# A hybrid backbone step on one core: the residual stored without its affine, modulation rows formed earlier, the last tile by halves

## The reference, cut to what matters

```python
x   = layer_norm(x, ln_in_g, ln_in_b)                       # input norm, with its affine
mod = silu(cond) @ w_mod + b_mod                            # six rows of 1024 per condition
shift1, scale1, gate1, shift2, scale2, gate2 = mod
u   = x * (1 + scale1) + shift1
x   = LN1(alpha * x + gate1 * TokenMix(u))                  # mLSTM + Fourier + pooling, merged, one output product
u2  = x * (1 + scale2) + shift2
x   = LN2(alpha * x + gate2 * HierMoE(u2))                  # top-1 group, top-2 of its 4 experts
```

## Time and profile before

| | us |
|---|---|
| median of 3 runs (1083.56, 1078.26, 1077.09) | 1078.26 |
| the profiled execution | 1081.63 |
| span of its trace | 1079.1 |
| PE busy (share of the span) | 998.3 (93%) |
| DVE busy | 664.8 (62%) |
| ACT busy | 445.4 (41%) |
| POOL busy | 172.2 (16%) |

### The profile page before, as it was taken

One profiled execution on the slowest core, in us unless ns is written; L12 is line 12 of the kernel. 1 busy time (PEld: TensorE's weight loads), 2 busy tenths in 40 slices (PEclk: granted clock), 3 DMA queues, 4 the chain that ended last, 5 costly groups with the idle time before them and its releaser, 6 DMA issues.

```text
span 1079.1 us, 13664 instructions
## 1 busy us (share of the span) xinstructions
PE 998.3 (93%) x4723; PEld 781.9 (72%) x4723; DVE 664.8 (62%) x943; ACT 445.4 (41%) x626; POOL 172.2 (16%) x210
## 2 busy tenths in 40 slices
PE   6997999999999999897989998699999999999883
PEld 2687998667777777764657776588888888888741
DVE  5569473024444547346486657786799955799628
ACT  1542221132443424301023013475688853778523
POOL 2133710111000001100212430311120101020030
PEclk6798998999999999998999998999999999999987
DMA  9856162241203102723354124695999988699572
GB/s 333 315 197 247 67 218 87 88 137 20 79 2 117 44 35 98 262 61 109 116 192 158 55 91 165 223 395 189 383 399 399 399 319 292 220 400 397 213 266 117
DMA packets 84967, 213.21 MB, mean 198 GB/s; under 512 B 7040, under 2 KB 7318, under 8 KB 84928
## 3 DMA queue, kind: packets, MB, share of 16 engines
q1 hardware_dynamic: 66000, 149.45, 37.8%
q0 software_dynamic: 14640, 48.51, 13.1%
q10 hardware_dynamic: 4288, 14.72, 3.6%
HBM read 189.54 MB, written 23.11 MB: 197 GB/s over the span
## 4 chain that ended last, share of the span: by engine, by line
PE 79%; DVE 9%; DMA 6%; ACT 3%; issue 2%; SPq 1%; ACTq 0%; POOL 0%; DVEq 0%
PE ps L1972 28%; PE ps L1734 22%; PE ps L1595 6%; PE ps L1720 5%; DMA ring<-in_w_in 2%; PE ps L1849 2%; PE ps L1966 1%; PE ps L1788 1%; DMA ring<-in_w_mod 1%; PE ps L1950 1%; PE ps L1601 1%; DVE w_lo L1169 1%; PE ps L1705 1%; ACT w_hi L848 1%; PE ps L1634 1%
## 5 line engine op out<-in xcount | busy, mean ns | idle before, releaser
L1734 PE MATMUL ps<-w_hi,uT_hi 128*128 128x512 f32 x320 | 132.9, 415 | 4.6 <-ACT R_x L913 2.5
L1734 PE MATMUL ps<-w_lo,uT_hi 128*128 128x512 f32 x320 | 126.7, 396 | 0.0
L1169 DVE TENSOR_TENSOR w_lo<-ring,w_hi 128x1024 fp32r<-128x1024 f32 x52 | 62.9, 1249 | 37.6 <-ACT w_hi L848 35.6
L1734 PEld LDWEIGHTS ps<-w_hi,uT_hi 128*128 128x128 f32 x320 | 60.9, 190 | 22.2 <-issue 5.4
L1408 DVE TENSOR_TENSOR wa_lo<-ring,wa_hi 128x1024 fp32r<-128x1024 f32 x64 | 74.1, 1218 | 0.5
L1734 PEld LDWEIGHTS ps<-w_lo,uT_hi 128*128 128x128 f32 x320 | 60.6, 190 | 13.5
L1972 PE MATMUL ps<-wa_hi,xgT_hi 128*128 128x512 f32 x152 | 62.8, 413 | 6.5 <-DVE xgT_lo L1505 6.5
L848 ACT CAST w_hi<-ring 128x1024 fp32r<-128x1024 f32 x52 | 53.0, 1059 | 34.0 <-PE ps L1734 23.4
L913 ACT ACTIVATE R_x<-ps 128x512 f32<-128x512 f32 x30 | 17.9, 596 | 116.0 <-PE ps L1734 115.9
L1734 PE MATMUL ps<-w_hi,uT_lo_a 128*128 128x512 f32 x160 | 64.1, 400 | 0.0
L1734 PE MATMUL ps<-w_hi,uT_lo_b 128*128 128x512 f32 x160 | 62.4, 390 | 0.0
(11 more groups left out here) (413 smaller groups left out, 2259.9 us busy)
## 6 DMA issues: line engine op xcount, KB each, us to landing
ring<-in_w_up SPq DMA_DIRECT2D x64, 512.0 KB, 9.5
ring<-in_w_in SPq DMA_DIRECT2D x11, 2048.0 KB, 10.1
R_d<-in_w_up SPq DMA_DIRECT2D x32, 512.0 KB, 10.9
R_p<-in_w_down SPq DMA_DIRECT2D x32, 512.0 KB, 9.7
R_h<-in_w_down SPq DMA_DIRECT2D x32, 512.0 KB, 10.3
y_slots<-R_m ACTq DMA_DIRECT2D x19, 512.0 KB, 6.2
ring<-in_w_mod SPq DMA_DIRECT2D x8, 1024.0 KB, 14.4
R_s<-in_w_up SPq DMA_DIRECT2D x16, 512.0 KB, 10.1
```

Source lines behind the costliest of these rows:

```text
L1169: tt(lo[:, at], weights(name)[:, at], hi[:, at].bitcast(F32), ALU.subtract).then_inc(S["w_split"], 1)
L1734: i = mm(out, parts(k)[a][:, tok(j)], w[b][:, k], start=(k == 0 and a + b == 0), stop=(k == KD - 1 and b == 1))
```

## The change

- x is stored without its affine. `spread_row`, `evict_rows`, `affine` and the loads of the two rows are gone. SP stores all five tiles of xn behind chunk "k", and ACT waits for these stores before it evicts k over them. The gate scans wait for xn instead of the stores. g and b come late, spread over partitions by POOL's queue, into buffers that are free by then, and DVE applies them (two instructions of 128x1024) in the output loop, before it takes the out product of that tile; SP's third weight piece of the second half waits until the last one is applied.
- Pieces 0 to 23 instead of 0 to 15 are formed around k, q and v; 24 to 31 go one to a merge step in steps 20 to 27. `sum_rows(0)` moves into q, `sum_rows(1)` and `sum_rows(2)` into v; the fold of the row for scale2 moves with them. POOL's loads stand between its pooling additions. The clearing of the pooling buffer and the store of zeros move ahead on POOL's list.
- In the front, PE gets 18 more idle products ahead of the modulation and groups of four between its halves.
- The last tile: out product, residual, statistics, u2, its transposes and logits go by halves of 512 columns (the logits of every tile start when the first half is evicted), 4 instead of 7 idle products stand before `route(4)`, and POOL finishes that tile's x ahead of the first gather, behind a wait for the second weight remainder of expert 0.
- The first expert tile: gathered rows are rounded by halves, DVE's subtraction goes ahead of the copy of the slots, and PE waits for each quarter of the weights instead of each half.

```diff
-                if name == "fp":
-                    for j in range(2):
-                        sp.wait_ge(S["x_ready"], j + 1)
-                        sp.dma_start(x_spill[tok(j), :], x_tok[:, j]).then_inc(S["x_spilled"], 16)
+                if name == "k":
                     sp.dma_start(consts[:, n0:], consts_d[:, n0:]).then_inc(S["consts_rest"], 16)
-                if name == "k":
-                    for j in range(2, NT):
-                        sp.wait_ge(S["x_ready"], j + 1)
-                        sp.dma_start(x_spill[tok(j), :], x_tok[:, j]).then_inc(S["x_spilled4"], 16)
-                    sp.wait_ge(S["x_spilled4"], 48)
+                    sp.wait_ge(S["xn_ready"], NT)
+                    for j in range(NT):
+                        sp.dma_start(x_spill[tok(j), :], xn_tok[:, j]).then_inc(S["x_spilled"], 16)
...
+            pool.wait_ge(S["xn_ready"], NT)
+            zp_clear = nc.gpsimd.memset(R_m[:, pad0:pad0 + 6 * PADW], 0.0)
...
+            load_mod_pieces(3, 8)
             chain(nc_t(sum_a[:, :, 1:W], zp_pad[:, :, 0:W - 1], zp_pad[:, :, 1:W], ALU.add))
+            load_mod_pieces(8, 10)
             chain(nc_t(sum_b[:, :, 2:W - 1], sum_a[:, :, 1:W - 2], sum_a[:, :, 3:W], ALU.add))
+            load_mod_pieces(10, 11)
...
-            load_mod_pieces(5, 16)
-            store_mod_row(0)
             pool.wait_ge(S["mod_stored"], 64)
             load_mod_bias(1)
+            load_mod_pieces(15, 24)
...
-                if j < NT - 1:
-                    first_norm_affine(j)
+                pool.wait_ge(S["x1_pre"], j + 1)
+                if j == NT - 1:
+                    pool.wait_ge(S["up_split"], 2)
+                first_norm_affine(j)
...
-            for i in range(4):
-                evict_rows(i)
             act.wait_ge(S["var_ready"], 1)
...
-            mod_pieces(0, 2)
+            mod_pieces(0, 3)
             split_chunk("k")
-            mod_pieces(2, 5)
+            mod_pieces(3, 8)
             split_chunk("q")
-            mod_pieces(5, 12)
+            mod_evict(0)
+            mod_pieces(8, 16)
             split_chunk("v")
-            mod_pieces(12, 16)
-            mod_evict(0)
+            was_read(dve, ("rowsum", 0))
+            mod_pieces(16, 24)
             mod_evict(1)
+            mod_evict(2)
...
+                if s < 28:
+                    mod_pieces(s + 4, s + 5)
...
+                ch(tt(x_tok[:, j], x_tok[:, j], g_in, ALU.mult))
+                tt(x_tok[:, j], x_tok[:, j], b_in, ALU.add).then_inc(S["x_restored"], 1)
...
+            for at in halves:
+                ch(stt(u2[j][:, at], rj[:, at], mean, ROW1["mul2_1"][:, at], ALU.subtract, ALU.mult), wait=False)
+            dve.wait_ge(S["std_ready"], j + 3)
+            ch(nc.vector.reciprocal(scale, scale))
+            for at, done in zip(halves, ("u2_half", "u2_ready")):
+                stt(u2[j][:, at], u2[j][:, at], scale, ROW1["add2_1"][:, at], ALU.mult, ALU.add).then_inc(S[done], 1)
...
             spread_positions(4)
+            idle_products(18, 0, P)
...
             modulation(0, 0)
+            idle_products(4, 2, P)
             modulation(0, 1)
-            spread_row(0)
-            spread_row(1)
+            idle_products(4, 2, P)
             fold_columns(0)
             modulation(1, 0)
-            spread_row(2)
-            spread_row(3)
+            idle_products(4, 2, P)
             modulation(1, 1)
-            idle_products(4, 5, P)
+            idle_products(4, 2, P)
...
+                    if part == "q" and c_ == 1:
+                        sum_rows(0)
...
+                if j == NT - 2:
+                    sum_rows(1)
+                    sum_rows(2)
...
             was_read(pe, ("out", NT - 2))
-            idle_products(7)
+            idle_products(4)
             route(NT - 1)
```

More of the change, by code:

```diff
@@ L117, in plan_psum @@
         fill(("modcol", c), "b3")
-        fill(("gb", c), ("b2", "p4")[c % 2])
     for d in range(KD):
@@ L131, in plan_psum @@
     fill("cols", "b2")
-    for v in range(2):
+    for v in range(3):
         fill(("rowsum", v), "p4")
@@ L668, in _ @@
             load_mod_bias(0)
[L669 to L672, removed]
+            load_mod_bias(2)
+            load_mod_pieces(3, 8)
             for c_ in (2, 3):
@@ L1203, in _ @@
             gate_rows(0, 0)
-            for j in range(2, NT):
-                affine(j)
             for s in (1, 0):
@@ L1615, in _ @@
             spread_positions(4)
+            idle_products(18, 0, P)
             fold = const("fold")
-            def spread_row(i_):
-                name = ("gb", i_)
-                begin(pe, name)
-                filled(mm(bank(gbank(name)), const("one")[0:1, :].to_broadcast([1, P]), gb_row[:, i_ * BW:(i_ + 1) * BW],
-                          start=True, stop=True), name)
             def modulation(c_, a):
@@ L1794, in _ @@
                 filled(i, name)
-            sum_rows(1)
             pe.wait_ge(S["pooled_ready"], 1)
@@ L1890, in _ @@
             for s in range(20, 30):
-                if s == 24:
-                    sum_rows(2)
                 merge_step(s)
@@ L1917, in route @@
                     filled(i, name)
-                for k in range(2):
-                    was_read(pe, ("uT2", j, k))
                 if j == 0:
                     begin(pe, "lg")
-                i = product(bank(1)[:, j * 20:(j + 1) * 20], "lg", lambda k: u2T[:, j % 2, k], lambda k: w_r[:, k], KD)
+                for k in range(KD):
+                    if k % 4 == 0:
+                        was_read(pe, ("uT2", j, k // 4))
+                    i = mm(bank(1)[:, j * 20:(j + 1) * 20], u2T[:, j % 2, k], w_r[:, k], start=(k == 0), stop=(k == KD - 1))
                 if j == NT - 1:
@@ L1981, in expert_tile @@
             def expert_tile(s, first=False, last=False):
-                pe.wait_ge(S["xgT_lo_ready"], s + 1)
                 if first:
-                    pe.wait_ge(S["up_split"], 4)
-                split_product(bank(0), xgT, wv_[0], KD).then_inc(S["up_full"], 1)
-                if first:
-                    pe.wait_ge(S["up_split"], 8)
-                else:
+                    for m in range(2):
+                        for k in range(KD):
+                            if m == 0 and k == 0:
+                                pe.wait_ge(S["xg_half_lo"], 1)
+                            if m == 0 and k == 4:
+                                pe.wait_ge(S["xgT_lo_ready"], 1)
+                            if k % 2 == 0:
+                                pe.wait_ge(S["up_split"], 4 * m + k // 2 + 1)
+                            for a, b in ((0, 0), (0, 1), (1, 0)):
+                                i = mm(bank(m), xgT[a][:, k * P:(k + 1) * P], wv_[m][b][:, k],
+                                       start=(k == 0 and a + b == 0), stop=(k == KD - 1 and a == 1))
+                        i.then_inc(S["up_full"], 1)
+                else:
+                    pe.wait_ge(S["xgT_lo_ready"], s + 1)
+                    split_product(bank(0), xgT, wv_[0], KD).then_inc(S["up_full"], 1)
                     pe.wait_ge(S["hidT_lo_ready"], s)
-                split_product(bank(1), xgT, wv_[1], KD).then_inc(S["up_full"], 1)
+                    split_product(bank(1), xgT, wv_[1], KD).then_inc(S["up_full"], 1)
                 if not last:
```

180 lines of the change are left out of this document (101 added, 79 removed).

## The result

The changed kernel took 1050.96 us as the median of four runs (1046.95, 1051.6, 1055.89, 1050.32), against 1078.4 before (one execution more than in the table ahead): a ratio of 0.9745, 95% interval 0.9703 to 0.9787. That is faster, and inside the range of 1030 to 1060; the forecast was 1044. The profiled execution took 1046.95 us (span 1044.9), the shortest of the four, while the profiled one of before was 0.3% above its median. On the profiled executions, on which the sum was made, the forecast was 1047.6.

What follows compares the result with a forecast made beforehand. PE, busy nine tenths of the span, was taken as the bound, with gains from its waits, removed work and half-clock stretches. Terms summed to -34: 1047.6 us for the profiled execution, 1044 as a median, range 1030 to 1060.

Steps and rivals of the forecast that it cites:

- (a): Front, up to the gate product `zg`: -8 us, with -10 at the higher clock and +2 for the clearing; bounds -11 to 0.
- half-clock rival: PE stays at the lower clock level in the front: 7 us worse, 1051; chance 0.16.
- (b): Split of chunk k: DVE loses three affines and the wait for x's stores; -10 us, bounds -10 and -6.
- (c): Eight more pieces between the splits of q and v stall the first v product: +5 us, bounds 0 and +12.
- (d): Row 2's pieces and sum leave the merge, with PE's wait of 6.4 us: -7 us, bounds -8 and -4.
- (e): End of the merge: w_out split runs ahead of step 29, wait of 4.7 falls to 0.4; -5 us, bounds -5 and -3.
- (f): Routing: five waits of 0.8 us for u2's second half shrink; -3 us, bounds -4 and -2.
- (g): Last tile: fewer idle products and work by halves bring transposes and logits earlier; -4 us, bounds -6 and -2.
- (h): POOL's affine of tile 4, moved ahead of the gather, runs beside DVE's routing chain: +3 us, bounds 0 and +4.7.
- (i): Start of the experts: PE's waits for the first and second tiles shrink; -5 us, bounds -7 and -1.
- the case in which all is covered: (c) and (h) cost nothing and (b), (g), (i) are at their best: 1030; chance 0.14.

Runs made afterwards that it cites:

- the second trace: The changed kernel run again, unedited, as the measure for the first group of edits: 1052.73 us, ratio 0.9746 against the kernel before.

## Why the prediction was right, and where it was not

**(a) Front: -8, measured -4.5.** Up to `zg` it was right to the tenth: xn written from 22.76, `zg` at 38.9 for a forecast of 39. The step that failed is the clearing: +2 of at most +3.5, measured +5.7 between `zg` and fp, outside its bounds, and 5.4 in time by the run that moved it. The bound was the clearing's own length, but the rounding was held for 6.2 us beyond its 0.42. Its recorded start lies 2.7 us before the clearing's; what held it in that time no run here shows. The Trainium skill (SBUF — State Buffer, "Who interferes with whom") was read too narrowly: beside the rule for two operands the same section says that copies and casts can run in a mode that uses both port pairs and contends with GpSimd, where whoever issues first gets the pair and the other blocks fully. This is a cast, beside a clearing, 6.59 instead of 0.42: the trace agrees that the two contend and one is held until the other ends, but not on the order, since by its recorded start the cast came first. So the sentence on record that by that page the term would be 0 was wrong. The clock, on which I hung the rest of the term, was 1.00 in this execution, as taken. Where it fell, `zg` came 1.0 us later (no idle products) or 4.1 later (lower level up to 40 us): the half-clock rival was a real one.

**(b) Chunk k: -10, right.** No wait of fp, k or q for a remainder; the 63.35 us from 60.13 to 123.48 run through. From fp to v 105.1 us became 101.8; without the 5.5 us of (c) and the 1.0 of the sum that now stands in q, that is 9.8 less.

**(c) +5: measured 5.5, 6 by the run that took it away.** The place, the releaser and the size were right, the mechanism to one half: the loads stood behind POOL's steps, and DVE's pieces were held by them, 3.42 and 4.07 us for 1.28. The load that DVE waited for last took 8.27 us, not 5.0; why is not shown.

**(d) -7 and (e) -5: measured -14.6** from the transposes before the merge to `merged`, with the stretch from v to the first unit 2.3 us longer (0.9 of it the wait between the two sums that now stand there). The net is 12.3, forecast 12. (e) alone is 4.2 in the waits and 7 in time by the run that undid it, with the clock behind it.

**(f), (g): -7 to the transposes of the last tile, measured -7.2** (653.1 - 563.8 = 89.3 before, 82.1 after). But not as put: the affine did not stay in idle time. DVE's 1.22 + 3.30 and a residual half of 2.03 kept u2 until just behind the idle products that are left, 0.3 us in PE's waits (1.4 in the second trace); without those products nothing was gained either.

**(h) +3: measured 4.0** (2.11 + 2.38 for 2 x 0.26), and 0.7 for a remainder ahead of the logits.

**(i) -5: measured -7.4** from the gather to expert 1, all but 1.5 of it between expert 0 and expert 1.

Not in the sum at all: 3.4 us behind expert 1, almost all in the last down product (5.04 for 6.65) and the last combine (7.12 for 8.82), at a granted clock of 1.00 in both where it was 0.75 and 0.81 before. The rows for this (chain; start, us, what), two of before and two of after:

```profile
1025.74 6.65 PE ps L2012 x21
1043.65 8.82 PE ps L2024 x16
```
```profile
995.00 5.04 PE ps L2042 x21
1011.16 7.12 PE ps L2054 x16
```

So the sum, 34 forecast and 34.2 measured on the profiled executions, is better than its terms, and by luck: (a) missed 3.5 and (h) 1 on one side, (i) 2.4 and the end 3.4 on the other, and the profiled execution was the fastest of ten of this kernel. Its second trace, at 1052.32 us, would have left 29 of the 34. The forecast took 0.3% off for the median, as in the kernel before; here the median lies 4 us above the profiled execution, and these two are the 7 us between 1044 and 1050.96. The last section tells how far executions of one kernel differ.

One sum on record does not come out: with (c) and (h) at nothing and (g) and (i) at their best the case in which all is covered gains 12 us, not 14, since (b) already stood at its best.

## What to carry to other kernels

A step that is moved on a second elementwise engine must be priced at every instruction of the first engine that will now run beside it: three such places stood beside a gain of 34 us in the profiled executions, and moving them by a few lines of one engine's list gave 11.7 more. An idle product, a late operand and a late weight can hide one another, so price what is second and third in line before counting a gain. In a sum that fits, look at the terms one by one: a right total can come from errors on both sides. A step that paces a stretch in one trace need not pace it in the next, when the clock has fallen: compare the stretch in several traces before calling a condition idle.

## What the runs showed of the hardware

- Two-operand instructions of 0.26 us on 100 elements took 2.11 and 2.38, about the length of POOL's instruction beside them (2.34 and 2.33), and two others in their place 2.14 and 2.26: the price there was what was left of the partner, not a share. A cast beside a clearing was held for longer than that, 6.2 us for a clearing of 3.60.
- The granted clock differs between executions of one kernel. The changed kernel's four runs had means of 0.972, 0.968, 0.964 and 0.969 for 1046.95, 1051.6, 1055.89 and 1050.32 us: the higher the mean, the shorter the run, over a range of 0.9%. In its six later runs the order is looser (0.972 for 1052.32, 0.969 for 1051.06). From 440 to 460 us, behind a wait of PE, the clock was 1.00 in both traces of the changed kernel and 0.91 in those without idle products ahead of the last routing and with the last three pieces behind step 28, whose lists differ from it only later; what decided it is not shown.
